# Second block of a two-block network: projections as three products of rounded parts and rests, by halves of K

## The chip, the cores and the metric

One program runs on one NeuronCore of a Trainium2 chip. The metric is the time of the whole program on the device in microseconds (us): the median of three runs is 1983.14 (1982.76 to 1983.52). One more execution was recorded by the profiler, and all rows below come from it. TensorE does the matmuls and transposes, VectorE (DVE) and ScalarE (ACT) the elementwise work, SyncE (SP) only issues transfers, and GpSimd (POOL) does nothing in the kernel before.

## The reference, cut to what matters

256 tokens of 1024 features go through a first block (attention, retention, an mLSTM, 16 experts; twice) and then through a second block, also two layers deep. The change is in the second block. One of its layers computes, in float32:

```
h   = rmsnorm(x, g_mix) @ w_in            # 1024 -> 2304, cut into
#     q, k (384 each: "aq", "ak"), v (384) and the window values (128): "avcv",
#     u and v of the gated unit (512: "buv"), window queries and keys (512: "cqk")
mix = [diff_attention(q, k, v), gmlp(u, v), window_attention(...)]   # 1024 wide
x   = x + rmsnorm(mix @ w_out, g_post)                               # "wo0", "wo1"
x   = x + rmsnorm((silu(h2 @ gate) * (h2 @ up)) @ down, g_post)      # 11 slices of 256
x   = x + rmsnorm(sigmoid(rmsnorm(x, g) @ w_gate) * (p @ w_up), g_post)  # "pg0", "pg1"
```

## The kernel before, in words

The kernel is written engine by engine: each engine has one queue of instructions in a fixed order, and they wait for each other through counting semaphores (`Done` counts them by name). Tokens are two chunks of 128 (t = 0, 1); the 1024 features are 8 steps of K. Weights come through two rings of buffers: `gring`, four slots of 8 x 520 values per partition, and `dring`, two slots of 2 x 1024 for the down weights. `ring_order` and `down_order` fix which chunk takes which slot; SyncE issues a transfer as soon as the last user of the slot's earlier chunk has finished (`free_slot`, `load_down`), in order.

There are two ways to multiply. `token_product` (L473, matmul L476) and `feature_product` (L487, matmul L490) take plain float32 operands: features `hT` and the weights as they landed. The first gives a chunk of tokens times 512 columns, the second 128 columns times all 256 tokens. The profile has two records for each of these matmuls. `split_product` (L480, matmuls L483 to L485) takes operands in two parts: a part rounded to the float32r type, and the rest, which is what is left after subtracting it. It adds three products, rounded x rounded, rounded x rest and rest x rounded, with one record each. It serves the gate, up and down weights of both blocks; ScalarE makes the rounded weights (`rounded_weights`, copy L1891), VectorE the rests in place (`weights_rest`, L1053), and the features go the same way (`features_rest`). The router's product (L836) has the same three parts.

A layer of the second block runs as follows (`pe_second` L869, `dve_second` L1626, `act_second`, `sp_second`). For each chunk the norm is taken (`pre_norm`), TensorE transposes it (L452), and VectorE (lower half) and ScalarE (upper half) scale it into `hT` (`modulated`, `modulated_T`). TensorE waits for both chunks. Then come aq (3 feature blocks), ak (3), avcv (2 token products), transposes of parameters, and the differential attention of 12 steps (`pe_attention`): in step s first a projection (`between_diff`: buv for s = 0, 1, cqk for s = 2, 3), then the scores of step s+3 (L922), then the transpose of the probabilities (L573) once VectorE has combined them (`diff_out`), then, after ScalarE's copy of it, the product with the values (L931). ScalarE also takes the exponentials, and one for lambda (`lsum`). The window attention has 6 steps. The mix is transposed (L468), ScalarE copies it to `hT`, and wo0 and wo1 are multiplied: (t0, wo0), (t0, wo1), (t1, wo0), the transposes of chunk 0's next norm, (t1, wo1). The 11 slices of the feed-forward part follow, with split products. Last stand the embedding product (L1016, buffer "up") and the ple gate: the norm of each chunk, transposes (L452), and four token products pg (L476). The next layer starts with the norm of the result.

## Time and profile before

| What | Value |
|---|---|
| median of 3 runs | 1983.14 us |
| the profiled execution: time, span | 1989.03 us, 1987.3 us |
| first block, to the last down product | to 1090.9 us |
| second block, layer 1: to the end of aq, ak, avcv | 1153.7 us |
| its first wo product, first slice of the feed-forward part | 1265.5 us, 1297.6 us |
| its embedding product, last pg product | 1493.1 us, 1537.1 us |
| second block, layer 2: aq to avcv | 1555.0 to 1591.5 us |

Times in the table are us from the start of the span, as in the rows. A row of a group of instructions gives busy time, the mean of one in ns, then the idle time of the engine just before them and who ended it. A row of the timeline gives start and duration in us, engine, line, operation, what it writes and reads, how many are merged into it, and in brackets the idle time before it. The duration of a matmul is longer than its distance to the next one; what counts for a sum is the distance.

### The profile page before, as it was taken

The numbers are of one execution on the slowest core, as the hardware profiler recorded it, in microseconds if no ns is written. First come the engines' busy times: TensorE is split into PE (matmuls) and PEld (weight loads), VectorE is DVE, ScalarE is ACT, GpSimd is POOL, SyncE is SP. The second block draws the span as 40 slices with busy tenths as digits, with TensorE's granted clock in tenths as the row PEclk, the third lists the DMA queues.
The fourth block names the chain that finished last, engine by engine and source line by source line (L and its number), as shares of the span: only waits on it lengthen the run. The fifth ranks groups of instructions, "written<-read, shape, count | busy, mean of one in ns | idle before, by whom it ended". The sixth has DMA issues, their size and how long they took to land.

```text
span 1987.3 us, 18106 instructions
## 1 busy us (share of the span) xinstructions
PE 1769.6 (89%) x6987; PEld 1253.1 (63%) x6987; DVE 1026.5 (52%) x1675; ACT 645.6 (32%) x1018; POOL 0.2 (0%) x4
## 2 busy tenths in 40 slices
PE   2999889999989889899999695899998786899996
PEld 2545558888864465678887453568884554478873
DVE  7564568667746345774444327244443146254433
ACT  1022344333411223334332124343334233343433
POOL 0000000000000000000000000000000000000000
PEclk8998799999989987899999796799999895899998
DMA  8663345877555330475554431035554440135540
GB/s 323 230 218 142 106 149 180 295 262 245 213 192 213 132 115 0 159 254 190 191 185 169 126 122 63 18 135 180 177 187 145 141 148 1 66 104 190 191 159 21
DMA packets 216373, 314.91 MB, mean 158 GB/s; under 512 B 20308, under 2 KB 145628, under 8 KB 216160
## 3 DMA queue, kind: packets, MB, share of 16 engines
q1 hardware_dynamic: 216288, 313.76, 46.0%
q8 instruction: 55, 0.90, 0.2%
q14 instruction: 30, 0.25, 0.0%
HBM read 312.70 MB, written 1.05 MB: 158 GB/s over the span
## 4 chain that ended last, share of the span: by engine, by line
PE 79%; DVE 13%; ACT 4%; issue 3%; SPq 0%; DVEq 0%; DMA 0%; ACTq 0%
PE psum L476 17%; PE psum L483 15%; PE psum L484 15%; PE psum L485 15%; PE psum L490 6%; DVE tmp L1056 3%; DVE arena L1056 2%; ACT arena L1891 1%; PE psum L526 1%; ACT arena L1888 1%; DVE arena L1053 1%; PE psum L452 1%; PE psum L931 1%; PE psum L961 1%; DVE arena L1300 1%
## 5 line engine op out<-in xcount | busy, mean ns | idle before, releaser
L476 PE MATMUL psum<-gring,hT 128*128 128x512 f32 (+1 forms) x960 | 433.8, 611 | 17.0 <-DVE arena L1053 6.1
L485 PE MATMUL psum<-arena_parts,hT_parts 128*128 128x512 f32 x864 | 344.2, 398 | 0.0
L476 PEld LDWEIGHTS psum<-gring,hT 128*128 128x128 f32 x960 | 189.6, 201 | 237.8 <-issue 213.6
L1053 DVE TENSOR_TENSOR gring_parts<-gring,arena_parts 128x2048 fp32r<-128x2048 f32 x108 | 242.7, 2289 | 99.0 <-ACT arena_parts L1891 99.0
L483 PE MATMUL psum<-arena_parts,o_cat_parts 128*128 128x512 f32 x512 | 205.2, 401 | 7.2 <-DVE hT_parts L1053 7.2
L484 PE MATMUL psum<-gring_parts,o_cat_parts 128*128 128x512 f32 x512 | 204.4, 399 | 0.0
L1053 DVE TENSOR_TENSOR arena_parts<-psum,ex_parts 128x256 fp32r<-128x256 f32 x108 | 45.3, 420 | 303.8 <-ACT ex_parts L1891 303.8
L1891 ACT ACTIVATE arena_parts<-gring 128x2048 fp32r<-128x2048 f32 x108 | 200.6, 1915 | 0.8 <-DMA gring<-in_w_up 0.7
L485 PEld LDWEIGHTS psum<-arena_parts,hT_parts 128*128 128x128 f32 x864 | 164.8, 191 | 39.1
L483 PE MATMUL psum<-arena_parts,ex_parts 128*128 128x512 f32 x432 | 180.4, 417 | 0.0
L1891 ACT ACTIVATE ex_parts<-psum 128x256 fp32r<-128x256 f32 x108 | 41.3, 382 | 416.2 <-PE psum L526 416.2
L485 PE MATMUL psum<-arena_parts 128*128 128x512 f32 x432 | 169.8, 393 | 0.0
L484 PE MATMUL psum<-dring_parts,ex_parts 128*128 128x512 f32 x432 | 169.7, 393 | 0.0
L1891 ACT ACTIVATE arena<-psum 128x512 f32<-128x512 f32 (+2 forms) x104 | 52.9, 511 | 301.3 <-PE psum L476 140.7
L483 PE MATMUL psum<-arena_parts 128*128 128x512 f32 x352 | 142.1, 404 | 4.5 <-DVE hT_parts L1053 4.5
L484 PE MATMUL psum<-gring_parts,arena_parts 128*128 128x512 f32 x352 | 140.4, 399 | 0.0
L1056 DVE SCALAR_TENSOR_TENSOR tmp<-gring,cact,tmp 128x512 f32<-128x512 f32 x168 | 126.3, 752 | 6.0
L1053 DVE TENSOR_TENSOR dring_parts<-dring,arena_parts 128x2048 fp32r<-128x2048 f32 x54 | 123.4, 2286 | 4.4 <-ACT arena_parts L1891 4.4
L490 PE MATMUL psum<-hT,gring 128*128 128x256 f32 (+1 forms) x512 | 121.7, 400 | 3.8 <-DVE small L1053 3.8
L483 PEld LDWEIGHTS psum<-arena_parts,o_cat_parts 128*128 128x128 f32 x512 | 97.7, 191 | 30.6 <-DVE hT_parts L1053 7.6
L490 PEld LDWEIGHTS psum<-hT,gring 128*128 128x128 f32 (+1 forms) x512 | 95.7, 189 | 27.9 <-issue 6.5
L484 PEld LDWEIGHTS psum<-gring_parts,o_cat_parts 128*128 128x128 f32 x512 | 97.9, 191 | 22.6
(207 smaller groups left out, 1889.7 us busy)
## 6 DMA issues: line engine op xcount, KB each, us to landing
gring<-in_w_ada SPq DMA_DIRECT2D x24, 2048.0 KB, 10.1
gring<-in_w_ffn_in SPq DMA_DIRECT2D x44, 1024.0 KB, 7.6
gring<-in_w_gate SPq DMA_DIRECT2D x32, 1024.0 KB, 7.5
gring<-in_w_up SPq DMA_DIRECT2D x32, 1024.0 KB, 9.9
dring<-in_w_down SPq DMA_DIRECT2D x32, 1024.0 KB, 5.1
gring<-in_w_in SPq DMA_DIRECT2D x14, 2048.0 KB, 10.8
dring<-in_w_ffn_out SPq DMA_DIRECT2D x22, 1024.0 KB, 4.9
gring<-in_w_out SPq DMA_DIRECT2D x8, 2048.0 KB, 8.8
```

Of the source, the lines that this page charges most:

```text
L452: last = nc.tensor.transpose((upper if k >= 4 else lower)[:, k % 4 * P:(k % 4 + 1) * P], src[:, t, k * P:(k + 1) * P], ident)
L476: last = nc.tensor.matmul(ps[:, 0:n], hT[:, k, t * P:(t + 1) * P], w[:, k, 0:n], start=k == 0, stop=k == KT - 1)
L483: nc.tensor.matmul(ps, hi, w, start=start, stop=False)
L484: nc.tensor.matmul(ps, hi, w_rest, start=False, stop=False)
L485: return nc.tensor.matmul(ps, lo, w, start=False, stop=stop)
L490: last = nc.tensor.matmul(ps[0:m, at:at + SEQ], w[:, k, c0:c0 + m], hT[:, k, :], start=k == 0, stop=k == KT - 1)
L526: last = nc.tensor.transpose(psum[:, 2 + t, f * P:(f + 1) * P], hid[:, t, f * P:(f + 1) * P], ident)
L931: last = nc.tensor.matmul(psum[:, 6 + t, h * HD:(h + 1) * HD], pT2[:, s % 2, k * P:(k + 1) * P], avcv[:, k, h * HD:(h + 1) * HD], start=k ...
L961: last = nc.tensor.matmul(psum[:, 6 + t, c:c + HD], pT2[:, s % 2, (h * TT + k) * P:(h * TT + k + 1) * P], avcv[:, k, 384 + h * HD:384 + (h ...
L1053: return nc.vector.tensor_tensor(o, a, b, op)
L1056: return nc.vector.scalar_tensor_tensor(o, a, s, b, op0, op1)
L1891: return nc.scalar.activation(o, a, ACT.Copy)
```

## The change

In the second block all projections become products of rounded parts and rests. Only the embedding product, attention and transposes stay.

- `half_tokens` and `half_features` do four of the eight steps of K, with three matmuls each. A chunk is rounded by halves: ScalarE copies the rounded half (`rounded_half`) to `dring_rest`, half 0 to the first down slot and half 1 to the second, which stand empty then; wo1 and pg1 use the second buffer of rounded gate weights instead. A half waits for the one that had the buffer before it (`rounded_before`). VectorE makes the rest in place (`chunk_rest`); for wo0 GpSimd does it, in 8 operations of 128 x 512 (`pool_second`).
- avcv is now the first chunk. Its first token chunk is multiplied as soon as chunk 0's features are there; the transposes of chunk 1 come behind it. Its weights are loaded ahead of the first block's last down weights.
- aq, ak, buv and cqk run by halves: first half of K for all outputs, then the second. In attention, buv's halves stand in steps 0 and 1, cqk's in steps 2 and 3.
- The features get a rounded part and a rest in all four places; the transposed mix is read by both ScalarE and VectorE, with four subtractions more.
- The first two down weights are loaded after the product (t1, wo0). The norm and the features of chunk 0 of the next layer are made between the steps of the ple gate.
- The features' rounded parts are laid out by token chunk in both blocks.

```diff
+IN_DOWN = ("avcv", "aq", "ak", "buv", "cqk", "wo0", "pg0")
+BY_POOL = ("wo0",)
...
+        def rounded_before(stage, name, q):
+
+            if name == "wo1":
+                return stage, T, ("win", "PV", len(WIN) - 1)
+            if name == "pg1":
+                return stage, T, ("gu1", NF - 2)
+            if name == "pg0":
+                return stage, T, ("e", 1, 1)
+            if name == "avcv":
+                return (FIRST[-1], T, ("dn1", NE - 2 + q)) if stage == SECOND[0] else (SECOND[0], T, ("pg", 1, 0))
+            return stage, T, ("half", IN_DOWN[IN_DOWN.index(name) - 1], q)
...
+        def half_tokens(ps, t, name, hi, q):
+
+            w, w_rest = rounded(name, q), g_rest(T.stage, name)
+            for k in range(4 * q, 4 * q + 4):
+                last = split_product(ps, hi[:, t, k, :], h_lo[:, k, t * P:(t + 1) * P], w[:, k % 4, :], w_rest[:, k, 0:N], k == 0, k == KT - 1)
+            return last
+
+        def half_features(ps, name, hi, c0, at, q, first, final):
+
+            w, w_rest = rounded(name, q), g_rest(T.stage, name)
+            o = ps[:, at:at + SEQ].rearrange("p (t n) -> p t n", t=TT)
+            for k in range(4 * q, 4 * q + 4):
+                nc.tensor.matmul(o, w[:, k % 4, c0:c0 + P], hi[:, :, k, :], start=first and k == 0, stop=False)
+                nc.tensor.matmul(ps[:, at:at + SEQ], w[:, k % 4, c0:c0 + P], h_lo[:, k, :], start=False, stop=False)
+                last = nc.tensor.matmul(o, w_rest[:, k, c0:c0 + P], hi[:, :, k, :], start=False, stop=final and k == KT - 1)
+            return last
...
             for t in range(TT):
                 transposed("xT", o_cat, t, 4 + 2 * t, ("xn", "mix", t))
...
+                wait_parts("hT", t)
+                for q in range(2):
+                    if t == 0:
+                        wait_weights("avcv", q)
+                    last = half_tokens(bank(T, ("avcv", t)), t, "avcv", h_hi[1], q)
...
+        def chunk_rest(stage, name, q, n=N):
+
+            k = slice(4 * q, 4 * q + 4)
+            dve.wait_ge(scalar_done, A.of(stage, ("hi", name, q)))
+            tt(g_rest(stage, name)[:, k, 0:n], gslot(stage, name)[:, k, 0:n], rounded(name, q)[:, :, 0:n], ALU.subtract).then_inc(vector_done, V.step(("lo", name, q), stage))
...
             if l == 0:
+                chunk_rest(stage, "avcv", 0)
+                joined(0)
+                scaled(0)
+                joined(1)
+                pre_norm("mix", 0)
+                scaled(1)
+                modulated("xT", "hT", 0, g_mix)
+                features_rest("hT", 0, h_hi[1])
+                chunk_rest(stage, "avcv", 1)
+                pre_norm("mix", 1)
             modulated("xT", "hT", 1, g_mix)
+            features_rest("hT", 1, h_hi[1])
+            for q in range(2):
+                chunk_rest(stage, "aq", q, 384)
+            for q in range(2):
+                chunk_rest(stage, "ak", q, 384)
...
+            chunk_rest(stage, "buv", 0)
             for s in range(3):
                 diff_in(s)
+            chunk_rest(stage, "buv", 1)
...
+                if s in (1, 2):
+                    chunk_rest(stage, "cqk", s - 1)
...
+            for q in range(2):
+                rounded_half(stage, "aq", q, 384)
+            for t in range(TT):
+                tokens("avcv", avcv, t)
+            for q in range(2):
+                rounded_half(stage, "ak", q, 384)
             for b in range(2):
                 features("aq", qT2, b, 2 - b, DQK ** -0.5)
+            rounded_half(stage, "buv", 0)
             for b in range(2):
                 features("ak", kT2, b, 2 - b)
+            rounded_half(stage, "buv", 1)
             act.wait_ge(vector_done, V.at(A, "lsum"))
             activate(lsum, lsum, ACT.Exp).then_inc(scalar_done, A.step("lexp"))
...
+                if s in (0, 1):
+                    rounded_half(stage, "cqk", s)
+                if s in (6, 7):
+                    rounded_half(stage, "wo0", s - 6)
...
+            for q in range(2):
+                rounded_half(stage, "pg0", q)
             for t in range(TT):
                 act.wait_ge(vector_done, V.at(A, ("x", "ffn", t)))
                 sum_squares(("pre", "ple"), t, x)
...
+                for k in range(4 * q, 4 * q + 4):
+                    nc.gpsimd.tensor_tensor(g_rest(stage, "wo0")[:, k, 0:N], gslot(stage, "wo0")[:, k, 0:N], rounded("wo0", q)[:, k % 4, :], ALU.subtract).then_inc(pool_done, Q.step(("lo", "wo0", q) if k % 4 == 3 else None))
```

## Rows read from the trace of the kernel before

**Rows 1.** The page: TensorE's busy time, and its granted clock by slices.

```profile
PE 1769.6 (89%) x6987; PEld 1253.1 (63%) x6987; DVE 1026.5 (52%) x1675; ACT 645.6 (32%) x1018; POOL 0.2 (0%) x4
...
PEclk8998799999989987899999796799999895899998
```

**Rows 2.** The chain of waits in order of time: start us, us, what.

```profile
811.83 3.08 PE psum L836 x24
...
1116.33 23.62 PE psum L490 x96
1139.95 13.75 PE psum L476 x32
...
1174.71 6.96 PE psum L490 x32
...
1290.75 6.88 PE psum L476 x16
...
1516.61 20.61 PE psum L476 x48
...
1577.74 13.75 PE psum L476 x32
```

**Rows 3.** A stretch by engines: busy time and records, then granted clock, DMA share, GB/s.

```profile
1308.00:1313.00 5.00, 4.71 (x11) 3.73 (x12) 2.71 (x4) 4.97 (x5) 0.00 (x0) 0.51 0.02 3
```

**Rows 4.** Timeline of TensorE: split products on either side of 1312.7 us.

```profile
1308.89 0.63 PE L484 MATMUL psum<-gring_parts,arena_parts 128*128 128x512 f32 x1
...
1312.30 0.63 PE L483 MATMUL psum<-arena_parts 128*128 128x512 f32 x1
...
1313.03 0.39 PE L485 MATMUL psum<-arena_parts,hT_parts 128*128 128x512 f32 x1
...
1315.82 0.39 PE L485 MATMUL psum<-arena_parts,hT_parts 128*128 128x512 f32 x1
```

**Rows 5.** The page's groups: rest of half a weight chunk, and its rounded copy.

```profile
L1053 DVE TENSOR_TENSOR gring_parts<-gring,arena_parts 128x2048 fp32r<-128x2048 f32 x108 | 242.7, 2289 | 99.0 <-ACT arena_parts L1891 99.0
...
L1891 ACT ACTIVATE arena_parts<-gring 128x2048 fp32r<-128x2048 f32 x108 | 200.6, 1915 | 0.8 <-DMA gring<-in_w_up 0.7
```

**Rows 6.** Timeline, all engines: entry of the second block's first layer.

```profile
1085.71 0.39 ACT L1891 ACTIVATE ex_parts<-psum 128x256 fp32r<-128x256 f32 x1 [2.56 <-PE psum L526]
...
1088.50 0.69 DVE L1053 TENSOR_TENSOR tmp<-psum,gb 128x512 f32<-128x512 f32 x1 [1.94 <-PE psum L485]
...
1103.30 2.49 DVE L1053 TENSOR_TENSOR x<-x,rows 128x1024 f32<-128x1024 f32 x2
...
1107.47 1.94 PE L452 MATMUL psum<-cshared,o_cat 128*128 128x128 f32 x8 [16.23 <-DVE o_cat L1049]
```

**Rows 7.** Timeline, all engines: from transposes of a chunk to its last rest.

```profile
1289.69 1.06 PE L452 MATMUL psum<-cshared,o_cat 128*128 128x128 f32 x8 [1.85 <-DVE o_cat L1049]
...
1292.24 1.29 DVE L1053 TENSOR_TENSOR hT_parts<-hT,arena_parts 128x512 fp32r<-128x512 f32 x2 [0.26 <-ACT arena_parts L1891]
```

**Rows 8.** Timeline: lambda's exponential; transposed probabilities of attention steps 0 and 3.

```profile
1141.74 0.20 ACT L1888 ACTIVATE small<-small 128x2 f32<-128x2 f32 x1
...
1163.97 0.44 PE L573 MATMUL psum<-cshared,arena 128*128 128x128 f32 x2
...
1191.38 0.44 PE L573 MATMUL psum<-cshared,arena 128*128 128x128 f32 x2
```

**Rows 9.** Timeline of TensorE: transposed probabilities of attention step 9.

```profile
1215.11 0.69 PE L573 MATMUL psum<-cshared,arena 128*128 128x128 f32 x2 [0.63 <-DVE arena L1056]
```

**Rows 10.** Timeline of TensorE: the first three wo products.

```profile
1265.50 22.34 PE L476 MATMUL psum<-gring,hT 128*128 128x512 f32 x48 [0.95 <-ACT hT L1891]
```

**Rows 11.** Timeline: ScalarE's sum of squares and TensorE's first product of the ple gate.

```profile
1500.69 1.05 ACT L1888 ACTIVATE arena<-x 128x1024 f32<-128x1024 f32 x1
...
1506.46 9.28 PE L476 MATMUL psum<-gring,hT 128*128 128x512 f32 x16 [1.34 <-DVE hT L1049]
```

More of the change, by code:

```diff
@@ L101, in ring_order @@
     for s in SECOND:
-        order += [(s, n) for n in ["aq", "ak", "avcv", "buv", "cqk", "wo0", "wo1"]]
+        order += [(s, n) for n in ["avcv", "aq", "ak", "buv", "cqk", "wo0", "wo1"]]
         order += [(s, f"gu{e}") for e in range(NF)] + [(s, "pg0"), (s, "pg1")]
@@ L872, in pe_second, with tokens @@
             turn[0] = 0
+            def tokens(name, q):
+                if q == 0:
+                    for t in range(TT):
+                        take((name, t), A)
+                wait_weights(name, q)
+                for t in range(TT):
+                    last = half_tokens(bank(T, (name, t)), t, name, h_hi[1], q)
+                    if q:
+                        last.then_inc(tensor_done, T.step((name, t)))
+                if q:
+                    T.also(("half", name, 1))
+                else:
+                    last.then_inc(tensor_done, T.step(("half", name, 0)))
@@ new lines, in features @@
+            def features(name, blocks, q):
+                if q == 0:
+                    for b in range(2):
+                        take((name, b), A)
+                wait_weights(name, q)
+                for f in range(blocks):
+                    last = half_features(bank(T, (name, f // 2)), name, h_hi[1], f * P, f % 2 * SEQ, q, f % 2 == 0, f in (1, blocks - 1))
+                    if q and f in (1, blocks - 1):
+                        last.then_inc(tensor_done, T.step((name, f // 2)))
+                if q:
+                    T.also(("half", name, 1))
+                else:
+                    last.then_inc(tensor_done, T.step(("half", name, 0)))
@@ L894, in parameters_T @@
+                last.then_inc(tensor_done, T.step(("avcv", t)))
+            T.also(("half", "avcv", 1))
             def parameters_T():
@@ L1790, in dve_second @@
             V.also("o_cat")
+            for g in range(KT // 2):
+                dve.wait_ge(scalar_done, A.at(V, ("oThi", g)))
+                ps = bank(V, ("oT", g)).rearrange("p (f t n) -> p f t n", f=2, t=TT)
+                for f in range(2):
+                    k = 2 * g + f
+                    tt(h_lo[:, k, :].rearrange("p (t n) -> p t n", t=TT), ps[:, f], h_hi[1][:, :, k, :], ALU.subtract).then_inc(vector_done, V.step(("oTlo", g) if f else None))
+                V.also(("read", ("oT", g)))
+            for q in range(2):
+                chunk_rest(stage, "wo1", q)
             weights_rest(0)
@@ L1799, in dve_second, with gate_weights @@
             modulated("xT2", "hT2", 1, g_ffn)
-            features_rest("hT2", 1)
-            dve_experts(NF, False, 1)
+            features_rest("hT2", 1, h_hi[1])
+            def gate_weights(e):
+                if e == NF - 1:
+                    for q in range(2):
+                        chunk_rest(stage, "pg1", q)
+            dve_experts(NF, False, 1, more=gate_weights)
             for t in range(TT):
@@ L1913, in modulated_T @@
             A.also(("read", (tag, t, 1)))
-            if parts:
+            if hi is not None:
                 for half in (1, 0):
@@ L2143, in act_second @@
             act.wait_ge(scalar_done, A.now())
-            for t in range(TT):
-                tokens("avcv", avcv, t)
             parameters_T()
@@ L2198, in act_second @@
                 act.wait_ge(tensor_done, T.at(A, ("oT", g)))
-                ps = bank(A, ("oT", g))
-                copy(hT[:, 2 * g:2 * g + 2, :].rearrange("p f n -> p (f n)"), ps).then_inc(scalar_done, A.step(("oTc", g)))
-                act.wait_ge(scalar_done, A.now())
-                A.also(("read", ("oT", g)))
+                ps = bank(A, ("oT", g)).rearrange("p (f t n) -> p f t n", f=2, t=TT)
+                for f in range(2):
+                    copy(h_hi[1][:, :, 2 * g + f, :], ps[:, f]).then_inc(scalar_done, A.step(("oThi", g) if f else None))
+            for q in range(2):
+                rounded_half(stage, "wo1", q)
             rounded_weights(0)
@@ L2296, in load_down, with load_first @@
             load(dslot(stage, name), src, DN.sem(stage, name))
+        def load_first(stage):
+            wi = layer("w_in_2", SECOND.index(stage))
+            free_slot(stage, "avcv")
+            for a, c0, n in ((0, 768, 384), (384, IN2 - P, P)):
+                load(gslot(stage, "avcv")[:, :, a:a + n], by_row(wi[:, c0:c0 + n]), G.sem(stage, "avcv"))
         def sp_first(l):
```

293 lines of the change are left out of this document (186 added, 107 removed).

## The prediction, made before the changed kernel ran

> **What bounds the kernel now.** I read the page first: TensorE is busy 1769.6 us of 1987.3, no other engine comes near it, and its granted clock is at 7 to 9 tenths from slice to slice, so not everywhere at full rate [rows 1]. Then the chain of waits, in order of time. In the second block it runs through the projection matmuls for tens of us (aq and ak together 23.62 us, avcv 13.75, each buv product about 6.9, each wo product 6.88, the last three ple gate products 20.6) [rows 2]; between these it leaves TensorE for VectorE and ScalarE. So a cheaper product shortens the kernel only where its operands are there in time. Everything after the first block's last expert differs; before that only one transfer is issued earlier and a layout changes.
>
> **Prices.** A token product (8 steps of K, 512 columns) is 16 records of plain f32, 6.88 us [rows 2]. The three-product form is there already in the gate and up weights: from 1313.03 to 1315.82 us lie 12 matmuls, 0.2325 us each, at the full 2.4 GHz; from 1308.89 to 1312.30 lie 8, 0.426 us each, at 1.2 GHz, and the stretch 1308 to 1313 is granted 0.51 on average [rows 3, 4]. 24 such matmuls are 5.57 us, 1.31 less than 6.88. A feature block (256 columns) is 16 f32 records, half of 6.96, so 3.48; the router's 24 matmuls of 256 columns take 3.08, tail included [rows 2], about 0.12 each, so 2.87 a block, 0.6 less. A layer has 12 token products (avcv 2, buv 2, wo 4, pg 4) and 10 feature blocks (3, 3, 4): 15.7 + 6 = 21.7 us less TensorE work, 43 in both layers. That is the ceiling.
>
> The price is paid elsewhere. Each half of a chunk wants a ScalarE copy of 128x2048 (1.9 us) and a VectorE subtraction (2.29 us) [rows 5], and for the 384-wide aq and ak three quarters of that (1.44 and 1.72). Nine chunks a layer: some 33 us of ScalarE, 35 of VectorE, 8 subtractions on GpSimd. Both engines have room on average; what matters is where each of these stands in its queue.
>
> **Entry, first layer of the block.** VectorE now first takes avcv's first rest: ScalarE is free at 1086.1, copy to 1088.05, rest to 1090.4, so the residuals start 1.9 us after their 1088.50 [rows 6]. The norm of chunk 0 is moved ahead of chunk 1's scaling (two row operations of 2.49, a scale of 0.8 and its reciprocal, with gaps 3.9 in all), so the transposes start at 1107.5 + 1.9 - 3.9 = 1105.5. But the lower half of their output waits for VectorE to end that scaling at 1108.9; modulation (1.15), copy (0.6) and rest (0.65) follow, and the first product starts at 1111.45 instead of 1116.33. After the long idle it runs 4.4 us at half rate, as from 1308.3 to 1312.7 [rows 4]: 7.6 us, to 1119.0. Only then do chunk 1's transposes come (in order on TensorE), and from transposes to both parts are 3.9 us, of which TensorE idles 2.9 (in the trace 1289.69 to 1293.53) [rows 7]. Product 1 would end at 1128.5. A gap like this can bring the clock down: after 1.85 us idle the transposes at 1289.69 still took 1.06 us [rows 7], but after two idle stretches of about 2 us the matmuls of 1308.89 ran at half rate [rows 4]. A drop would cost about 1.7; I take 1.25. aq's first weights wait until that half buffer is free (middle of product 1), then 1.6 + 1.8 us: it starts at 1130.3. Six blocks at 2.87 are 17.2: projections end at 1147.6, before at 1139.95 + 13.75 = 1153.7 [rows 2]. **Gain 5.9.** The rests of aq's second half and of ak arrive 1 to 2 us early behind 4.3 us of products: they cost nothing, and 1 to 2 us if VectorE were late.
>
> **Start of attention, per layer.** Now ScalarE's queue has, behind the end of ak: ak's last copy, buv's second half (1.9), then the table load and exponential of lambda (1.5; before, it was done at 1141.94, long before it was wanted) [rows 8]. VectorE waits for that exponential ahead of buv's first rest: it gets it 4.4 us after ak's end, and the rest ends at 6.75. TensorE has 3 us of transposes and scores and idles 3.9. buv's first half (24 matmuls) starts 6.85 after ak's end, after that gap partly at half rate: 7.5, then a score step 0.7: first probabilities' transpose 15.1 us after ak's end. VectorE alone (three score steps 4.1, buv's second rest 2.3, its output step 1.3) would give 14.5. Before it was 10.4 (1153.7 to 1163.97, in the rows) [rows 8]. **Loss 4.6**, the largest single one.
>
> **The four steps with a projection between.** Before, 27.4 us from the first of these transposes to the fourth (1163.97 to 1191.38) [rows 8], three intervals of 9.14. After, TensorE needs 1.47 + 5.57 or 5.76 + 0.7, so 7.7 to 7.9. In the first two, VectorE is later: output and score step, 1.1 of exponentials, copy 1.9, rest 2.29, output step 1.3 give 8.2 and 8.05. The third is 7.9. **Gain 3.2**.
>
> **wo0's rounding.** Two copies of 1.9 us fall between the exponentials of steps 6 and 7, where ScalarE is free for less than that in a step: 0.5 lost. The 8 GpSimd subtractions (128x512 each) have no row: there is no GpSimd tensor work in the trace. They are wanted 50 us later, so their own length is covered; the question is whether they hold up VectorE while they run beside it. Bounds: nothing, or their whole time, which at VectorE's own price (a quarter of 2.29) is 8 x 0.57 = 4.6 us a layer [rows 5]. VectorE has only 0 to 0.5 us of slack there: in step 9 TensorE waits 0.63 for it [rows 9], while before steps 10 and 11 it is 1 to 1.5 us early. I take 1.5 a layer, a third of the bound, since three of VectorE's six operations in a step read two operands from SBUF. **Loss 2.0.**
>
> **wo.** Transposed outputs now need two copies and two subtractions per bank, and the third and fourth bank wait for VectorE: parts are complete at 1268.0 where the product started at 1265.50 [rows 10]: 2.5 lost. Two products give back 2.8 (a start at half rate is in both), so +0.3. The product after the next transposes gains 1.45, but the idle ahead of it grows from 1.85 to 3.15 us; I take 1.3 for a clock drop. **Gain 0.45.** wo1's rounding lies under wo0's product; first down weights are loaded only after wo: 5 us for a need 15 us later, hidden.
>
> **ple gate.** pg1's rests delay the last expert's down product by 0.5. pg0's two copies (3.7 us) stand on ScalarE ahead of the sum of squares at 1500.69 [rows 11] because their buffer is free only then. With 0.6 from before: sum of squares at 1505.05, transposes at 1508, modulated at 1511.15, pg0's first rest (2.29), then the features' rests (1.3): the first gate product starts at 1514.9 instead of 1506.46 [rows 11], 8.4 late. The old one took 9.1 us to the next transposes; now 7.6, then three of 5.57, against 20.61 before [rows 2]. Last product ends at 1540.1, before at 1537.1. **Loss 3.0**, and in the last layer this is the kernel's tail.
>
> **Entry, second layer.** On from 1540.1: ScalarE goes through two avcv copies and three table loads, VectorE through two rests: first product 1551 to 1558.6, chunk 1's norm is ready at 1558.9, product 1 from 1562.9 to 1569.8 (clock allowance in), aq from 1570.2, projections end 1587.4; before 1577.74 + 13.75 = 1591.5 [rows 2]. **Gain 4.1**, the ple loss of the first layer included.
>
> **Sum.** First layer 5.9 - 4.6 + 3.2 - 2.0 + 0.45 = 2.95. Second 4.1 - 4.6 + 3.2 - 2.0 + 0.45 = 1.15, tail -3.0. Together 1.1 us. The profiled execution took 1989.03 (span 1987.3), so 1987.9; the median of the runs shown is 5.9 lower, and taken from it the forecast is 1982.0. Of 43 us of cheaper products nearly all goes into waits for rounded parts.
>
> **Rivals.** (A) *GpSimd stalls VectorE fully*: each of 8 subtractions holds back a VectorE operation of output steps 8 to 11, one after another, and takes longer than VectorE's 0.57. If 4.5 us a layer is lost rather than 1.5, the time is 1982 + 6 = 1988, slower. For it: VectorE has no slack in step 9 [rows 9]. Against: no row shows a stall. It decides from 4.05 us a layer. The Trainium skill (SBUF, State Buffer, Who interferes with whom) states this as an exclusive lock of a port pair between GpSimd and VectorE operations with two SBUF inputs, and its GPSIMD Engine Reference (Performance versus the Vector engine) gives 4497 ns for 2048 f32 elements beside 2293 on VectorE; an estimate by that page is 1.12 us an operation, 9 us a layer. The 2293 agrees with the 2.29 here; the lock no run here shows. (B) *The gaps are cheap*: no GpSimd stall (3.0) and the clock stays up in the four gaps where I took 1.25 or 1.3 (5.1): 1973.9. For it: 1.85 us idle left the clock up [rows 7]. Against: my gaps are 2.9 and 3.15. (C) *It doesn't do what it says*: TensorE waits in each chunk for the rest of a half, 1 us for each of 18: near 1999. Against: the rests come early behind aq and ak.
>
> **How the numbers follow.** Forecast 0.45, A 0.25, B 0.25, C 0.05. Predicted 1982.0. The range goes to A with some room above and B with some below, 1972 to 1990, C left out. What can be told from no change is 0.2%, 4 us: 1979.2 to 1987.1. Faster: B and a part of the forecast's spread, 0.32. Slower: most of A, and C, 0.25. Same 0.43.
>
> **What would show it.** In the changed profile: token product 5.6 us at full clock; projections ending 6 us earlier in the first layer; TensorE idle 4 us before buv's first half with VectorE behind the exponential; attention steps 1 to 3 at 8 us; GpSimd at work in steps 7 to 10 and VectorE's small operations in that stretch with gaps of 0.5 us or more (A) or without (B); wo starting 2.5 us later after the last output norm; first ple gate product 8 us later after the last expert. It is wrong if the lambda exponential is not in the way, if 256-column matmuls of strided halves run slower than the router's 0.12, or if a transfer lands late.

## The result and the profile after

The changed kernel takes 2000.44 us (median of 4 runs, 1998.23 to 2001.66). Beside it the kernel before took 1983.33; the ratio is 1.008 (95% interval 1.0062 to 1.0098): slower by 0.8%, clear of the interval. The forecast of 1982.0 and its range to 1990 are both missed. The profiled execution took 1999.85 us, span 1998.0. Its page, busy TensorE and the clock granted to it in 40 slices:

```profile
PE 1741.2 (87%) x7339; PEld 1298.7 (65%) x7339; DVE 1119.6 (56%) x1739; ACT 720.6 (36%) x1080; POOL 20.8 (1%) x20
...
PEclk9998699999989988899999785699998885799997
```

TensorE is busy 28 us less than in [rows 1], VectorE 93 more and ScalarE 75 more, and yet the span is 10.7 us longer: the products got cheaper and the waits dearer. The ends of the stages of the second block come out of TensorE's timeline. Here are the rows of after that open or close them in the first layer: last product of the first block, first parameters' transposes, first, fourth and tenth transpose of probabilities, first gate product.

```profile
1089.09 0.40 PE L538 MATMUL psum<-arena_parts 128*128 128x512 f32 x1
...
1146.88 0.60 PE L980 MATMUL psum<-cshared,arena 128*128 128x128 f32 x4
...
1162.27 0.44 PE L626 MATMUL psum<-cshared,arena 128*128 128x128 f32 x2
...
1189.61 0.44 PE L626 MATMUL psum<-cshared,arena 128*128 128x128 f32 x2
...
1217.76 0.69 PE L626 MATMUL psum<-cshared,arena 128*128 128x128 f32 x2 [2.86 <-DVE arena L1138]
...
1518.60 0.77 PE L536 MATMUL psum<-dring_parts,arena_parts 128*128 128x512 f32 x1 [4.89 <-DVE hT_parts L1135]
```

The same marks in both traces give this table (us; change: plus is slower; the forecast's terms from its own sum):

| Stage | before | after | change | forecast |
|---|---|---|---|---|
| layer 1: last expert product to parameters' transposes | 62.27 | 57.39 | -4.88 | -5.9 |
| to first transpose of probabilities | 10.45 | 15.39 | +4.94 | +4.6 |
| to the fourth | 27.41 | 27.34 | -0.07 | -3.2 |
| to the tenth | 23.73 | 28.15 | +4.42 | +2.0 |
| to the first transpose of the mix | 44.49 | 44.49 | 0 | 0 |
| to the embedding product (wo, feed-forward) | 233.53 | 235.47 | +1.94 | -0.45 |
| to the end of the last gate product | 44.08 | 46.08 | +2.00 | +3.0 |
| layer 2: to parameters' transposes | 54.10 | 48.05 | -6.05 | -7.1 |
| to first transpose of probabilities | 10.44 | 16.35 | +5.91 | +4.6 |
| to the fourth | 27.41 | 26.82 | -0.59 | -3.2 |
| to the tenth | 23.99 | 28.14 | +4.15 | +2.0 |
| to the first transpose of the mix | 44.50 | 44.50 | 0 | 0 |
| to the embedding product | 235.16 | 234.31 | -0.85 | -0.45 |
| to the end of the last gate product | 44.17 | 45.87 | +1.70 | +3.0 |
| to the end of the span | 10.32 | 10.16 | -0.16 | 0 |

The whole second block went from 896.05 to 908.51 us: 12.5 slower where 1.1 less was forecast. The forecast of -7.1 for layer 2's entry is the gain of 4.1 that the sum has, with the 3.0 us of the gate ahead of it taken out, since they have their own row. In the traces the first block, which the change hardly touches, ended at 1091.25 before and at 1089.49 after.

### The profile page after: what moved, and what is told of

It reads as the page before. It is cut to its first block, busy times and chain, and to the rows that moved or that the text cites. A ratio compares the mean times of both kernels' runs of the same rounds, so it can differ in the third digit from the quotient of the medians.

```text
span 1998.0 us, 18986 instructions
## 1 busy us (share of the span) xinstructions
PE 1741.2 (87%) x7339; PEld 1298.7 (65%) x7339; DVE 1119.6 (56%) x1739; ACT 720.6 (36%) x1080; POOL 20.8 (1%) x20
## 4 chain that ended last, share of the span: by engine, by line
PE 75%; DVE 15%; ACT 5%; issue 4%; SPq 0%; DVEq 0%; ACTq 0%; DMA 0%
PE psum L536 17%; PE psum L537 17%; PE psum L538 17%; PE psum L501 9%; DVE tmp L1138 3%; PE psum L543 2%; DVE arena L1138 2%; PE psum L579 1%; ACT arena L2034 1%; ACT arena L2037 1%; DVE arena L1135 1%; DVE gring_parts L1135 1%; PE psum L477 1%; PE psum L522 1%; PE psum L523 1%
## 5 line engine op out<-in xcount | busy, mean ns | idle before, releaser
L538 PE MATMUL psum<-arena_parts,hT_parts 128*128 128x512 f32 x928 | 370.6, 399 | 0.0
L1135 DVE TENSOR_TENSOR gring_parts<-gring,arena_parts 128x2048 fp32r<-128x2048 f32 x116 | 260.4, 2287 | 85.8 <-ACT arena_parts L2037 85.8
L501 PE MATMUL psum<-gring,hT 128*128 128x512 f32 (+1 forms) x576 | 256.2, 603 | 12.4 <-DVE arena L1135 6.1
L537 PE MATMUL psum<-gring_parts,arena_parts 128*128 128x512 f32 x544 | 224.9, 413 | 0.0
L2037 ACT ACTIVATE arena_parts<-gring 128x2048 fp32r<-128x2048 f32 x116 | 215.3, 1916 | 0.1
L538 PEld LDWEIGHTS psum<-arena_parts,hT_parts 128*128 128x128 f32 x928 | 177.8, 192 | 42.3
L501 PEld LDWEIGHTS psum<-gring,hT 128*128 128x128 f32 x576 | 113.6, 201 | 140.0 <-issue 121.6
L536 PE MATMUL psum<-arena_parts 128*128 128x512 f32 x416 | 168.0, 404 | 4.5 <-DVE hT_parts L1135 4.5
L538 PE MATMUL psum<-arena_parts 128*128 128x512 f32 x432 | 169.8, 393 | 0.0
L537 PEld LDWEIGHTS psum<-gring_parts,arena_parts 128*128 128x128 f32 x544 | 109.2, 201 | 24.6
L2037 ACT ACTIVATE arena_parts<-dring 128x2048 fp32r<-128x2048 f32 x54 | 103.3, 1913 | 0.0
```

The lines of the kernel that those rows point to most:

```text
L501: last = nc.tensor.matmul(ps[:, 0:n], hT[:, k, t * P:(t + 1) * P], w[:, k, 0:n], start=k == 0, stop=k == KT - 1)
L536: nc.tensor.matmul(ps, hi, w, start=start, stop=False)
L537: nc.tensor.matmul(ps, hi, w_rest, start=False, stop=False)
L538: return nc.tensor.matmul(ps, lo, w, start=False, stop=stop)
L1135: return nc.vector.tensor_tensor(o, a, b, op)
L2037: return nc.scalar.activation(o, a, ACT.Copy)
```

## Experiments

Times called "second block" below run from the end of the first block's last product to the end of the span of the profiled execution.

**The kernel before, and the changed kernel, once more.** 

> The kernel before once more, nothing changed, for a second trace. Its profiled execution took 1989.03 us while the median of its runs was 1983.1. If the extra 5.9 us lie in single transfers or waits, this trace shows a span nearer to 1981.5 and the difference has a place; if a profiled execution is always longer, the span is again about 1987. The distance from the first score step's projection to the end of attention should be the same within 0.3 us in both.

> The changed kernel once more, nothing edited, beside the kernel before on the same chip. If the stages are as reproducible as they were in the two traces of before (895.9 and 896.1 us from the last product of the first block to the end), the second block takes 908.5 us within 0.5 again, and only the first block's end moves, between 1085 and 1094 us; the median then lies 10 to 15 us above that of before.

Before again: 1991.41 us, span 1989.6, second block 895.92 us; after again: second block 908.57, median 1999.62 over 1985.67, ratio 1.0066 (1.0046 to 1.0086). Every stage of the table came back within 0.1 us, so stages are compared below even where a kernel has one trace only (the roundings first, roundings and banks, two GpSimd operations). What moves is the first block. The last product of the first block in before again, and TensorE's windows over the first 250 us (busy times, then granted clock, DMA share, GB/s) of before again and of the changed kernel with lambda first (below), whose first block ended at 1085.27:

```profile
1093.28 0.40 PE L485 MATMUL psum<-arena_parts 128*128 128x512 f32 x1
```

```profile
0.00:250.00 250.00, 197.59 (x684) 117.49 (x685) 149.26 (x337) 47.55 (x99) 0.20 (x4) 0.87 0.57 203
```

```profile
0.00:250.00 250.00, 197.63 (x702) 118.06 (x703) 149.25 (x337) 49.11 (x102) 0.20 (x4) 0.92 0.57 203
```

The same engines are as busy, at a granted clock of 0.87 and 0.92, and the block ends 8 us apart. On one chip 28 runs of the kernel before took 1982.3 to 1991.9 us, median 1988.0. So the three runs first shown lay at the lower edge, and the profiled 1989.03 was an ordinary run. The clock of these 250 us does not order the traces alone: with 0.92 the first block ended at 1085.3 to 1085.7 us in four of them, but with 0.90 at 1089.5 and at 1093.1.

**GpSimd's subtractions given to VectorE.**

```diff
-BY_POOL = ("wo0",)
+BY_POOL = ()
@@ VectorE, behind the last diff_out @@
+            for q in range(2):
+                chunk_rest(stage, "wo0", q)
```

> The changed kernel with wo0's rests taken by VectorE (two operations of 128x2048, 2.29 us each) right behind the last step of the first attention, instead of by GpSimd in eight operations; ScalarE's roundings stay where they are. Theory (GpSimd's operations hold back VectorE's with two operands in SBUF): the stretch from the fourth probabilities' transpose to the tenth falls from 28.15 back to about 23.7 us, and since VectorE idled 4.45 us where the two rests now stand, 0 to 0.5 us a layer is lost there: 8 to 9 us faster than the changed kernel, about 1991.5 to 1992.5. Rival (the steps are late because of ScalarE's two roundings between the exponentials): those stay, so nothing is gained and the rests cost up to 4.6 us a layer: 2000 to 2005.

Measured: fourth to tenth transpose 24.32 and 24.31 us instead of 28.15 and 28.14; second block 898.34, 10.2 us less than after. Its median of 1989.26 stands to before as 1.0004 (0.999 to 1.0018), where after stands at 1.0066. ScalarE's two roundings are still there, so they were not the main cause; 0.6 and 0.3 us a layer are left over before. VectorE's two rests stand behind the tenth transpose, in a stretch that took 44.4 us with and without them. The 2.5 us beyond the two stretches fell mostly out of the entry of layer 2 (43.54 from its first transposes instead of 45.74), where less ran at half rate: the granted clock over the entry was 0.89 instead of 0.82. What the hold-up looks like in the changed kernel, on VectorE, with GpSimd's row first:

```profile
1208.51 10.32 POOL L2457 TENSOR_TENSOR gring_parts<-gring,dring_parts 128x512 fp32r<-128x512 f32 x8 [1208.07 <-ACT dring_parts L2037]
```

```profile
1205.43 0.16 DVE L1135 TENSOR_TENSOR small<-small 128x1 f32<-128x1 f32 x1
1205.63 0.35 DVE L1131 TENSOR_SCALAR arena<-arena,small 128x256 f32<-128x256 f32 x1
1206.02 0.48 DVE L1138 SCALAR_TENSOR_TENSOR arena<-arena,small 128x256 f32<-128x256 f32 x1
...
1209.05 0.75 DVE L1135 TENSOR_TENSOR small<-small 128x1 f32<-128x1 f32 x1
1209.84 1.32 DVE L1131 TENSOR_SCALAR arena<-arena,small 128x256 f32<-128x256 f32 x1
1211.19 1.38 DVE L1138 SCALAR_TENSOR_TENSOR arena<-arena,small 128x256 f32<-128x256 f32 x1
1212.60 0.69 DVE L1138 SCALAR_TENSOR_TENSOR arena<-cblock,psum 128x512 f32<-128x512 f32 x1
1213.32 0.69 DVE L1794 TENSOR_REDUCE small<-arena 128x2 f32<-128x512 f32 x1
1214.04 0.17 DVE L1799 RECIPROCAL small<-small 128x2 f32<-128x2 f32 x1
```

The first three rows are an output step without GpSimd, the next three one beside it: 0.16, 0.35 and 0.48 us became 0.75, 1.32 and 1.38. The busy time swells, there is no idle gap to see. The reduction, the reciprocal and the operation that reads PSUM keep their 0.69 and 0.17. Of the six operations the three that grew read all they need from SBUF, two tensors or a tensor and a scalar for each partition.

**The same elements in two GpSimd operations.**

```diff
-                for k in range(4 * q, 4 * q + 4):
-                    nc.gpsimd.tensor_tensor(... 128x512 ...)
+                k = slice(4 * q, 4 * q + 4)
+                nc.gpsimd.tensor_tensor(... 128x2048 ...)
```

> The changed kernel with GpSimd's eight subtractions of 128x512 merged into two of 128x2048: the same elements, two operations. Theory (a VectorE operation with two operands in SBUF waits for the end of the GpSimd operation under way): each now lasts about 5 us, VectorE passes only between the two and behind the second, a single VectorE operation shows up to 5 us, and the stretch from the fourth to the tenth transpose of probabilities, 28.15 us in the changed kernel and 24.3 with the rests on VectorE, grows to 30 to 33: 2 to 5 us a layer slower. Rival (both engines share the memory's bandwidth, each operation is only stretched in proportion): the stretch stays within 0.5 us of 28.15.

Measured: 31.35 us in both layers (28.15 and 28.14 in after), second block 915.46. GpSimd's row, then VectorE's:

```profile
1209.79 8.97 POOL L2457 TENSOR_TENSOR gring_parts<-gring,dring_parts 128x2048 fp32r<-128x2048 f32 x2 [1209.34 <-ACT dring_parts L2037]
```

```profile
1210.12 0.17 DVE L1799 RECIPROCAL small<-small 128x2 f32<-128x2 f32 x1
1210.33 3.99 DVE L1135 TENSOR_TENSOR small<-small 128x1 f32<-128x1 f32 x1
1214.36 4.55 DVE L1131 TENSOR_SCALAR arena<-arena,small 128x256 f32<-128x256 f32 x1
1218.94 0.48 DVE L1138 SCALAR_TENSOR_TENSOR arena<-arena,small 128x256 f32<-128x256 f32 x1
```

An operation on one element a partition takes 3.99 us: it ends when GpSimd's first does, and the next when the second does. GpSimd was even busy less (8.97 against 10.32 us), and VectorE lost more. It is a lock held for a whole operation, not a shared bandwidth. The Trainium skill (SBUF, State Buffer, Who interferes with whom) states this contention as an exclusive lock. These rows agree with it.

**Lambda's exponential first.**

```diff
+            act.wait_ge(vector_done, V.at(A, "lsum"))
+            activate(lsum, lsum, ACT.Exp)...
             rounded_half(stage, "buv", 0)
             for b in range(2):
                 features("ak", kT2, b, 2 - b)
             rounded_half(stage, "buv", 1)
-            act.wait_ge(vector_done, V.at(A, "lsum"))
-            activate(lsum, lsum, ACT.Exp)...
             parameters_T()
```

> The changed kernel with lambda's exponential moved ahead of both roundings of buv on ScalarE; nothing else. Theory (attention starts late because VectorE waits for that exponential ahead of buv's first rest): the exponential runs at about 1142.3 to 1143.8 in the changed kernel's times, buv's first rest ends by 1148.5 instead of 1153.87, and buv's first half starts when the third score step is out, about 1151.5 instead of 1154.57: 3 us a layer, 6 in all, about 1994.5; the parameters' copies behind buv's second rounding are then what is late. Rival (two banks are asked for at once and VectorE's first score steps free them late): the start stays at 1154 and the time at 2000.

Measured: second block 901.73, 6.8 less than after; parameters' to first probabilities' transpose 13.90 and 12.39 instead of 15.39 and 16.35, so 5.5 of the 6.8 us are this stretch. The rest is no part of the theory: 0.5 us in the four steps and 0.7 in the wo stage of layer 1 are most of it. Of its 11 runs the median is 1996.79, the ratio to before 1.0037 (1.0022 to 1.0053). In after, ScalarE, VectorE and TensorE:

```profile
1147.66 1.91 ACT L2037 ACTIVATE dring_parts<-gring 128x2048 fp32r<-128x2048 f32 x1
1149.59 1.28 ACT L2034 ACT_TABLE_LOAD   x1
1150.88 0.20 ACT L2034 ACTIVATE small<-small 128x2 f32<-128x2 f32 x1
```

```profile
1151.19 0.35 DVE L1135 TENSOR_TENSOR small<-small 128x1 f32<-128x1 f32 x2 [8.58 <-ACT small L2034]
1151.58 2.29 DVE L1135 TENSOR_TENSOR gring_parts<-gring,dring_parts 128x2048 fp32r<-128x2048 f32 x1
1153.79 0.68 DVE L1138 SCALAR_TENSOR_TENSOR arena<-cblock,psum 128x512 f32<-128x512 f32 x1
```

```profile
1152.35 1.22 PE L1000 MATMUL psum<-arena 32*128 32x256 f32 x4 [3.79 <-ACT arena L2037]
1154.57 0.77 PE L536 MATMUL psum<-dring_parts,arena_parts 128*128 128x512 f32 x1 [1.00 <-DVE arena L1138]
```

And in the edited kernel, VectorE and TensorE:

```profile
1141.87 2.29 DVE L1135 TENSOR_TENSOR gring_parts<-gring,dring_parts 128x2048 fp32r<-128x2048 f32 x1 [1.70 <-ACT dring_parts L2037]
```

```profile
1146.51 1.22 PE L1000 MATMUL psum<-arena 32*128 32x256 f32 x4 [2.13 <-ACT arena L2037]
1147.66 0.80 PE L536 MATMUL psum<-dring_parts,arena_parts 128*128 128x512 f32 x1
```

VectorE's 8.58 us of idle end with the exponential, as forecast. In after the rest is over at 1153.87, and buv's first product starts at 1154.57, when VectorE's first score step has read its bank: so the rival's bank is there too, but worth 0.7 us, and the start did not stay. buv's first half starts 4.97 us behind the parameters' transposes instead of 7.69. In the first layer half of the gain was given back: its 24 matmuls took 8.4 us against 7.1 in after (5.6 at full rate); in the second layer they took 7.4 against 8.1, and there 4.0 us were gained. Next in the way is the third score step, which still waits 2.13 us for the parameters' copies on ScalarE.

**The gate's first chunk in other buffers.**

```diff
+            if name == "pg0":
+                return (d_hi[1], dring_rest[:, 0])[q]...
-                return stage, T, ("e", 1, 1)
+                return stage, T, ("dn1", NF - 2 + q)
@@ ScalarE: q = 0 behind the last expert's hidden copies, q = 1 behind modulated_T of chunk 0 @@
@@ VectorE: chunk_rest(stage, "pg0", 0) ahead of modulated("xT3", "hT3", 0, g_ple) @@
```

> The changed kernel with pg0's rounded halves in buffers that are free earlier: the first half takes the rounded down weights' second buffer (free when the last expert but one is through) and is rounded behind the last expert's hidden copies, the second takes the first down buffer and is rounded behind the first chunk's modulation; the squares' scratch moves out of their way, and VectorE takes the first rest while the transposes run. Theory (two roundings ahead of the sum of squares make the gate product late): from the start of the embedding product to the first gate product 14 to 15 us instead of 20.9, the last gate product 5 to 6.5 us earlier in each layer: 10 to 13 us faster, 1987.5 to 1990.5. Rival (VectorE's queue of rests is the limit, which has the same length): 2.3 us a layer at most, 1995.5 to 2000.

Measured: embedding product to first gate product 13.53 us (1493.94 to 1507.47) instead of 20.88, in the kernel before 13.33; second block 894.61, 13.9 less than after; ratio to before 0.9992 (0.9978 to 1.0006). This one stretch, from the embedding product to the end of the last gate product, is 7.1 and 7.2 us shorter in the two layers, in sum more than the whole loss. TensorE's timeline of this kernel, where the idle time ahead of the transposes is 1.65 us; the last row is from after, where it was 7.02 us:

```profile
1502.62 1.06 PE L479 MATMUL psum<-cshared,o_cat 128*128 128x128 f32 x8 [1.65 <-DVE o_cat L1133]
1507.47 0.76 PE L538 MATMUL psum<-arena_parts 128*128 128x512 f32 x1 [3.79 <-DVE hT_parts L1137]
```

```profile
1511.77 1.94 PE L477 MATMUL psum<-cshared,o_cat 128*128 128x128 f32 x8 [7.02 <-DVE o_cat L1131]
```

Ahead of that row VectorE itself stood idle for ScalarE's sum of squares, with no rest in its queue:

```profile
1510.12 0.15 DVE L1132 TENSOR_SCALAR small<-small 128x1 f32<-128x1 f32 x1 [5.40 <-ACT arena L2034]
```

Of the 7.35 us by which the first gate product comes earlier, 5.4 lie ahead of the transposes, so they are the roundings'. The other 2.0 lie behind them; there VectorE's first rest was moved too, and the transposes took 1.06 instead of 1.94 us. How the 2.0 are shared was not tested.

**The four steps: which wait stands between the products.** First ScalarE's order, then that and the banks.

```diff
+                if s in (0, 1):
+                    rounded_half(stage, "cqk", s)
                 if s + 3 < len(DIFF):
                     diff_exp(s + 3)
-                if s in (0, 1):
-                    rounded_half(stage, "cqk", s)
```

```diff
                 elif s < 4:
                     features("cqk", 4, s - 2)
+                if s in (1, 3):
+                    turn[0] = 4
```

> The changed kernel with cqk's two roundings ahead of the exponentials of score steps 3 and 4 on ScalarE instead of behind them; nothing else. In the changed kernel ScalarE's copy (1.91 us) and VectorE's rest (2.29) then stand 2 us earlier. Theory of the prediction (the chain exponentials, copy, rest, output step sets the intervals between probabilities' transposes at 8.2 and 8.05): the first interval falls from 8.69 by about 0.5, the second from 8.46 by 0.5. Rival (the score step behind each product waits for ScalarE to read the product's banks, 0.84 and 0.75 us in the trace, and a part of the third product runs at half rate): the first interval stays at 8.69, the second falls by the 0.47 us for which the transpose waited for VectorE, the third stays at 10.2 or 8.7. Four steps together: 26.3 to 26.9 us by either, the split decides.

> As the run with the roundings first, and the score steps behind the second half of buv and of cqk take another pair of banks, whose readers are long through, instead of the pair that holds the projection just computed. Theory (the bank waits of 0.84 and 0.75 us stand on the path once VectorE is early): the three intervals become about 7.85, 8.0 and 8.0 at full rate (9.4 where the third product is at half rate), the four steps together 24 to 25.5 instead of 27.3 and 26.8 us. Rival (TensorE waits next for VectorE's output step): the bank waits turn into waits for VectorE and the sum stays above 26.3.

The three intervals between the first four transposes of probabilities:

| Kernel | layer 1 | layer 2 | second block |
|---|---|---|---|
| after | 8.69, 8.46, 10.19 | 8.69, 9.44, 8.69 | 908.51 |
| rounding first | 8.70, 7.92, 8.72 | 8.69, 9.48, 8.72 | 905.22 |
| and banks | 7.79, 7.92, 7.90 | 7.79, 7.91, 7.90 | 901.82 |

Rows of after ahead of the second and fourth transpose, then of the kernel with both edits ahead of the fourth, then the third interval of layer 1 as a window in after and with the rounding first (busy times, then granted clock, DMA share, GB/s):

```profile
1170.33 0.70 PE L1000 MATMUL psum<-arena 32*128 32x256 f32 x4 [0.84 <-ACT arena L2037]
...
1188.97 0.70 PE L1000 MATMUL psum<-arena 32*128 32x256 f32 x4 [0.75 <-ACT arena L2034]
```

```profile
1189.69 0.70 PE L1000 MATMUL psum<-arena 32*128 32x256 f32 x4
1190.32 0.44 PE L626 MATMUL psum<-cshared,arena 128*128 128x128 f32 x2
```

```profile
1179.42:1189.61 10.19, 8.97 (x59) 8.19 (x59) 2.52 (x6) 2.67 (x7) 0.00 (x0) 0.83 0.03 4
```

```profile
1175.01:1183.73 8.72, 7.45 (x61) 6.67 (x59) 2.54 (x6) 2.67 (x7) 0.00 (x0) 1.00 0.02 5
```

The rival is right for the first and third interval: a score step takes a pair of banks and gets the one that holds the projection just finished, so it waits for ScalarE's copy of it. VectorE's chain was late in the second interval alone, by 0.54 us in layer 1. The rest of the excess is half rate: 1.5 us in the third interval of layer 1 (10.19 against 8.72), gone without an edit to it once the times ahead of it had shifted, and 1.5 in the second interval of layer 2, which went when the banks were changed. In after the granted clock of that interval of layer 2 was 0.82. Free of both waits the three come to 23.6 us, below the forecast's 24.2. Each of the two kernels ran once, in 1992.59 and 1997.49 us: the second was the longer one only because its first block ended 8.3 us later.

**All five edits together.** 

> The changed kernel with five edits: wo0's rests on VectorE, lambda's exponential ahead of buv's roundings and the parameters' copies ahead of buv's second, pg0's halves in earlier buffers, cqk's roundings ahead of the exponentials, and free banks for two score steps. From the end of the first block's last product to the end the changed kernel took 908.5 us, the kernel before 896.0. If the gains seen alone add up (10.2, 6.8 and 13.9 us) and the steps give another 3 to 6 and the earlier third score step 1 to 2: 870 to 874 us, that is 22 to 26 us less than before: ratio to before 0.987 to 0.989, about 1963 to 1966 us where before takes 1988. Rival (the gains overlap, and cheaper waits bring longer stretches at half rate): 878 to 884, ratio 0.991 to 0.994.

Measured: second block 863.89 us; median 1955.15 (1950.42 to 1958.28), ratio to before 0.9834 (0.9815 to 0.9853). That is more than the rival and more than the sum: 44.6 us less than after, and 1.7% faster than the kernel before. The sum of what was seen alone is 10.2 + 6.8 + 13.9 + 6.7 = 37.6. The rest is mainly the start of attention, 9.31 us in both layers where the kernel before took 10.45: 13.1 us less than after in the two layers, where lambda alone had brought 5.5. With the parameters' copies ahead of buv's second rounding the third score step waits 0.25 us instead of 3.79, and the product behind it runs at full rate (1145.49 to 1151.24). The parameters' order was not run alone. TensorE's timeline of this kernel:

```profile
1144.86 0.70 PE L1002 MATMUL psum<-arena 32*128 32x256 f32 x4 [0.25 <-ACT arena L2043]
1145.49 0.50 PE L538 MATMUL psum<-dring_parts,arena_parts 128*128 128x512 f32 x1
```

**Is the split of wo worth it?** In the fast kernel wo became a plain product again, without roundings and rests (some 30 lines, as in the kernel before).

> The kernel with all five edits, in which wo stays a plain f32 product: no roundings, no rests, the mixed outputs copied once. With the split, the stretch from the first transpose of the mixed outputs to the second chunk's transposes ahead of the experts took 43.4 and 46.2 us in the two layers, in the kernel before 45.4 and 46.5. The prediction gave the split of wo a gain of 0.45 us a layer there and a price of 0.5 on ScalarE, so next to nothing in sum. By that the second block stays at 863.9 us within 1.5. Theory of a real gain (wo's 5.2 us of cheaper products count, since the queues are free by then): 3 us or more a layer are lost, 870. Rival (the split of wo costs more than it gives, as the 1.9 us lost in the changed kernel's first layer suggest): 860 to 862.

Measured: second block 867.16, 3.3 us more in two layers; median 1958.58, ratio 0.9855 (0.9834 to 0.9876). None of the three: the split of wo is worth 1.6 us a layer on average, with its price in attention (0.64 and 0.28 us) taken off. The stretch from the mix's first transpose to the embedding product is 3.7 us longer in layer 1 and 0.1 in layer 2, so the gain is not the same in both layers. Up to the second chunk's transposes ahead of the experts the split takes 43.43 and 46.21 us at a granted clock of 0.87 and 0.82, plain wo 46.77 and 46.18 at 0.88 and 0.89: the clock takes the gain back in layer 2.

## Why the prediction was wrong

By its own steps:

- **Prices of products: right.** avcv's first product took 7.4 us with a start at half rate (7.6 forecast), aq and ak 17.25 from first to last (17.2), free products between the steps 7.8 to 7.9 an interval.
- **Entry: mostly right.** Transposes 13.92 us after the last expert product (14.25 forecast), first product at 20.15 (20.2). The second product began at half rate after a gap of 2.89 us and took 8.5 us where 5.57 and an allowance of 1.25 were taken; aq's start, forecast 0.6 us behind that product's end for its own weights, hid a part, and 1 us of the gain went in each layer. In after, the timeline's row with the gap, and the window behind it (last three numbers: granted clock, DMA share, GB/s):

```profile
1120.80 0.76 PE L536 MATMUL psum<-dring_parts,arena_parts 128*128 128x512 f32 x1 [2.89 <-DVE hT_parts L1135]
```

```profile
1120.00:1125.00 5.00, 4.20 (x10) 3.36 (x11) 0.69 (x2) 0.00 (x0) 0.00 (x0) 0.50 0.00 0
```

- **Start of attention: mechanism and size right in layer 1** (4.94 against 4.6), 1.3 too small in layer 2, where buv's first half started as early (7.69 us behind the parameters' transposes) but took 8.1 us instead of 7.1, more of it at half rate. The idle time forecast as one stretch of 3.9 us is two, 3.79 ahead of the third score step and 1.00 behind it: the queue ahead of the parameters' copies was overlooked.
- **Four steps: the first wrong term**, 3.2 us a layer against 0.07 and 0.59. The sum "1.47 + 5.57 + 0.7" left out that a score step needs a pair of banks, and the change makes two projections' banks end together at the end of a half. Beyond the 23.6 us of the run that is free of these waits, after takes 3.7 in layer 1 (banks 0.9 and 0.8, VectorE 0.5, half rate 1.5) and 3.2 in layer 2 (banks 0.9 and 0.8, half rate 1.5). The forecast stood 0.5 us above the 23.6 itself, for VectorE, so the term was off by 5.7 us in both layers together, the largest part of the error: 3.4 us of banks and 3.0 of half rate are not in it, and 0.6 of what it allowed for VectorE was not used.
- **GpSimd: the second wrong term**, 2.0 forecast, 4.42 and 4.15 measured. The 0.5 in it for ScalarE's roundings held (0.6 and 0.3 measured with the rests on VectorE). The 1.5 for GpSimd did not: 3.8 us a layer are GpSimd's. Rival A, at 0.25, had the mechanism; in size 3.8 lies between the forecast's 1.5 and A's 4.5, and below the 4.05 from which A alone would have decided. "Three of six operations read two operands" was true and was used to cut the bound to a third, but these three stand one behind another on the path, and each waits for the end of an operation of 1.29 us. VectorE's price for an operation, 0.57, was too low by more than half. That the bound made of it, 4.6, still lay above the 3.8 is luck: GpSimd was busy 10.3 us a layer, and it held up three operations in each of two output steps for whose end TensorE waited. The estimate from the Trainium skill (GPSIMD Engine Reference, Performance versus the Vector engine), 1.12 an operation, was the nearer one: its 4497 ns for 2048 elements agree with 8.97 us for two here.
- **wo: +1.94 and -0.85** against -0.45 and -0.45, 1.5 of the 2.8 us between the layers being the rate (16.97 and 15.47 us between the two transposes ahead of the experts, 15.3 before). The product started 2.0 us later after the mix's transposes, forecast 2.5, and the first of these two transposes came 0.55 and 0.87 us earlier, forecast 0.3. (By the prediction's own price of 1.31 a product its "2.8" for two should read 2.6.) What failed is the stretch behind it in layer 1.
- **Gate: too dark.** 2.00 and 1.70 where 3.0 was taken, 7.5 us late at the first product where 8.4 was; cause as forecast: the run with other buffers takes 5.4 us out ahead of the transposes, where only the roundings stood.
- **The anchor.** From the profiled 1989.03 the terms gave 1987.9; 5.9 was taken off to meet the median of three runs. The error in the second block is 13.6 us (1.1 + 12.5): entries 2.1, starts of attention 1.7, four steps 5.7, steps beside GpSimd 4.6, wo 2.0, less 2.3 of the gate and 0.2 at the end. A first block that ended 1.8 us earlier by luck works against it, so that 1999.85 - 1987.9 = 12.0 is left (the marks are read to 0.1 us). Another 5.9 of the 18.4 us is the anchor, chosen from too few runs; the last 0.6 is the median over the profiled run. The range was built around it and lacked these 5.9 us, too; with them, to 1996, it would still have missed.

Rival C, at 0.05, named a time near 1999, and the measured 2000.44 lies beside it by coincidence. Its mechanism did not happen: in the whole second block the rest of a weight half was what a product waited for last only twice, 1.2 us together, where C had 18 us. Elsewhere the rests and roundings cost time by standing ahead of other work in a queue. The row of TensorE's waits in after (total us, times, longest):

```profile
PE psum L522 <- DVE gring_parts L1135: 1.2, 2, 0.8
```

Two readings of the prediction are loose. The page's granted clock also has a slice at 6 and one at 5 tenths. And the "two idle stretches of about 2 us" ahead of 1308.89 are not in rows 4; in the trace they are 1.80 and 2.24 us.

The chances had A and the gaps apart, with all other terms at their value. Each term was a best guess with the waits seen so far. What was overlooked (banks, an operation held for GpSimd's whole operation, half rate in more places) all added time, and the range gave that little room.

## What to carry to other kernels

When products get cheaper by work moved to other engines, count for each product what its start needs: operands, but also its banks and the buffers that the new copies want, and look in each engine's queue for a short step that has landed behind a long one. Five such edits turned a change that costs 12.5 us into one that gives 32. Compare traces by stages between marks of the same work, which came back within 0.1 us here, while the whole moved by 9 us for a reason outside the change.

## What was not expected of the hardware

- A VectorE operation held back by GpSimd shows as a long operation, not as idle time: 3.99 us for 128x1 elements. A 128x2048 f32 subtraction on GpSimd took 4.5 us (8.97 for two), eight of 128x512 took 1.29 each, 10.32 in all.
- The first block, in which the experiments' edits change nothing, ends between 1085.3 and 1093.9 us in the 12 traces of this case, with the granted clock in its first 250 us between 0.87 and 0.92. Two traces of one kernel, before and before again, are 2.4 us apart in it. Why the clock differs from run to run is not shown.
- Half rate moves: the third interval above lost 1.5 us in one kernel and not in the next (granted clock 0.83 and 1.00), though neither its work nor the wait in it, 0.75 us, had changed. What brought it there in single cases stays open; no run here was made on that alone.
